# Delta rule: where the inverse's transposed first value is made, and the order of two VectorE steps

## The reference, cut to what matters

```
L = where(strict, (k_beta @ k.T) * decay, 0)
T = triangular_solve(eye + L, eye)                # the inverse of I + L
v_corr = T @ v_beta
k_cumdecay = T @ (k_beta * exp(gc))
attn_intra = where(tril, (q @ k.T) * decay, 0)
# scan over chunks: state, o
o_gdn = rms_norm(o, gdn_out_norm_w) * silu(z)     # the gated output
```

```
qkv = silu(sum(xp[:, i:i+S] * w[i] for i in range(4)))
```

## Time and profile before

| | |
|---|---|
| median of 3 runs | 2905.5 us (2904.29 to 2907.15) |
| profiled execution | 2909.46 us, its span 2907.7 us |
| PE busy | 2759.3 us (95%) |
| DVE busy | 1890.3 us (65%) |
| ACT busy | 1195.7 us (41%) |
| POOL busy | 536.7 us (18%) |
| delta rule | from about 300 to 690 us of the span |

### The profile page before, as it was taken

The page is one execution under the profiler, slowest core; times in us unless marked ns, Lnnn a source line. Parts: engine busy times, 40 slices in busy tenths (PEclk is TensorE's granted clock), DMA queues, the critical chain, the costliest instruction groups (busy, mean ns, idle before and its releaser), DMA issues.

```text
span 2907.7 us, 36988 instructions
## 1 busy us (share of the span) xinstructions
PE 2759.3 (95%) x14045; PEld 2343.5 (81%) x14045; DVE 1890.3 (65%) x3534; ACT 1195.7 (41%) x1928; POOL 536.7 (18%) x393
## 2 busy tenths in 40 slices
PE   8999999989998999999998999999999978999997
PEld 6777878878777999998997888888887546788876
DVE  3334665765565778877975888888885674544434
ACT  5545243233223454447993333333333444422322
POOL 0112220220000787771000111111110021000000
PEclk9999999999999999999999999999999989999999
DMA  4112101003562587765768989998883101222220
GB/s 160 51 51 86 60 30 44 30 30 131 217 217 114 201 300 280 271 236 191 284 231 308 336 319 346 337 350 324 334 304 131 30 30 44 80 97 92 87 102 29
DMA packets 141359, 501.19 MB, mean 172 GB/s; under 512 B 13400, under 2 KB 67072, under 8 KB 111616
## 3 DMA queue, kind: packets, MB, share of 16 engines
q1 hardware_dynamic: 122752, 364.60, 35.0%
q0 software_dynamic: 18432, 134.23, 11.8%
HBM read 450.53 MB, written 48.25 MB: 172 GB/s over the span
## 4 chain that ended last, share of the span: by engine, by line
PE 80%; DVE 9%; ACT 5%; DMA 3%; issue 2%; POOL 1%; SPq 0%; DVEq 0%; ACTq 0%; POOLq 0%
PE bank L244 21%; PE bank L246 21%; PE bank L245 21%; PE bank L2154 2%; DVE xn L1532 1%; PE bank L2743 1%; PE bank L1107 1%; PE bank L740 1%; PE bank L1117 1%; PE bank L1123 1%; DMA w_raw<-in_w_in_dram 1%; DVE M L2946 1%; DVE m L2942 1%; PE bank L346 1%; DVE whl L240 1%
## 5 line engine op out<-in xcount | busy, mean ns | idle before, releaser
L244 PE MATMUL bank<-HH,uhl 128*128 128x384 f32 x1024 | 349.9, 342 | 9.0 <-DVE uhl L1658 7.1
L246 PE MATMUL bank<-HH,uhl 128*128 128x384 f32 x1024 | 346.7, 339 | 0.0
L245 PE MATMUL bank<-HL,uhl 128*128 128x384 f32 x1024 | 346.6, 339 | 0.0
L244 PE MATMUL bank<-vhl,awhl 128*128 128x512 f32 x768 | 300.0, 391 | 6.7 <-DVE awhl L2372 4.7
L246 PE MATMUL bank<-vhl,awhl 128*128 128x512 f32 x768 | 299.8, 390 | 0.0
L245 PE MATMUL bank<-vhl,awhl 128*128 128x512 f32 x768 | 299.5, 390 | 0.0
L1714 POOL DMA_INDIRECT gs<-in_uv_dram,idx x128 | 151.6, 1185 | 776.0 <-DVE x L1739 481.6
L2312 ACT ACTIVATE vhl<-vraw 128x1024 fp32r<-128x1024 f32 x128 | 135.7, 1061 | 317.3 <-PE bank L246 281.8
L1658 POOL TENSOR_TENSOR uhl<-ur,uhl 128x1024 fp32r<-128x1024 f32 x69 | 167.7, 2439 | 321.1 <-ACT uhl L1652 320.8
L244 PE MATMUL bank<-HH,whl 128*128 128x512 f32 x528 | 215.8, 409 | 5.9 <-DVE whl L240 4.1
L240 DVE TENSOR_TENSOR whl<-w_raw,whl 128x2048 fp32r<-128x2048 f32 x49 | 113.5, 2317 | 160.2 <-ACT whl L234 160.1
(11 more groups left out here) (421 smaller groups left out, 6197.3 us busy)
## 6 DMA issues: line engine op xcount, KB each, us to landing
ur<-in_peer_u_dram SPq DMA_DIRECT2D x128, 512.0 KB, 5.5
vraw<-in_peer_v_dram SPq DMA_DIRECT2D x128, 512.0 KB, 5.9
w_raw<-in_w_in_dram SPq DMA_DIRECT2D x36, 1024.0 KB, 5.0
xn<-in_ada_rows_dram SPq DMA_DIRECT2D x48, 512.0 KB, 4.5
g_scratch<-stg SPq DMA_DIRECT2D x12, 2048.0 KB, 8.1
gti<-g_scratch SPq DMA_DIRECT2D x16, 1536.0 KB, 11.5
wf_raw<-in_f_w_in_dram SPq DMA_DIRECT2D x22, 1024.0 KB, 4.8
act_scratch<-ag SPq DMA_DIRECT2D x96, 192.0 KB, 2.7
```

The source lines that it names most:

```text
L244: e.matmul(out, l[0], r[0], start=start, stop=False)
L245: e.matmul(out, l[0], r[1], start=False, stop=False)
L246: return e.matmul(out, l[1], r[0], start=False, stop=stop)
```

## The change

XT's first value is no longer made from LT by GpSimd. In step 3 PE transposes X into a bank of the ring, behind the product of the same head, and ScalarE copies it into XT. GpSimd's two operations for it are gone. The wait for "onw" moves to ScalarE, and step 4's first product waits for ScalarE. In VectorE's order, the first convolution of the next pair goes from step 1 to step 2, behind the six evictions; the gated outputs of the pair before go from step 2 to step 4, behind the updates of X and XT.

```diff
--- before.py
+++ after.py
@@ -1106,8 +1106,15 @@
                 for tb in range(NT):
                     i = e.matmul(b[:, blk(tb)], B["LT"][:, tb, :], B["X"][:, tb, :], start=True, stop=True)
                 i.then_inc(*T.up("p", h, l))
+                if l == 0:
+                    b = R3.take("xT", h)
+                    for s in R3.empty("xT", h):
+                        e.wait_ge(*s)
+                    for tb in range(NT):
+                        i = e.transpose(b[:, blk(tb)], B["X"][:, tb, :], ident)
+                    i.then_inc(*T.up("xT", h))
             else:
-                e.wait_ge(*(V.of("xt", h, l - 1) if l else G.of("XT", h)))
+                e.wait_ge(*(V.of("xt", h, l - 1) if l else A.of("xT", h)))
                 e.wait_ge(*V.of("p", h, l))
                 if l < LV - 1:
                     b = R3.take("x", h, l)
@@ -1176,6 +1183,11 @@
         if seg == 1:
             e.wait_ge(*T.of("lt", h))
             e.activation(B["LT"][:, :, :], in4(R3.bank("lt", h)), ACT.Copy).then_inc(*R3.out(A, "lt", h))
+        if seg == 3:
+            if h >= 2:
+                e.wait_ge(*V.of("onw", h - 2))
+            e.wait_ge(*T.of("xT", h))
+            e.activation(B["XT"][:, :, :], in4(R3.bank("xT", h)), ACT.Copy).then_inc(*R3.out(A, "xT", h))
         if seg == 15:
             e.wait_ge(*T.of("vc", h))
             e.activation(B["L"][:, :, :], in4(R3.bank("vc", h)), ACT.Copy).then_inc(*R3.out(A, "vc", h))
@@ -1274,13 +1286,6 @@
             e.tensor_tensor(B["X"][:, :, :], B["L"][:, :, :], cb("neg1"), ALU.mult).then_inc(*G.up("x0", h))
             e.wait_ge(*G.of("x0", h))
             e.tensor_tensor(B["X"][:, :, :], B["X"][:, :, :], cb("ident"), ALU.add).then_inc(*G.up("X", h))
-        if seg == 1:
-            e.wait_ge(*A.of("lt", h))
-            if h >= 2:
-                e.wait_ge(*V.of("onw", h - 2))
-            e.tensor_tensor(B["XT"][:, :, :], B["LT"][:, :, :], cb("neg1T"), ALU.mult).then_inc(*G.up("xt0", h))
-            e.wait_ge(*G.of("xt0", h))
-            e.tensor_tensor(B["XT"][:, :, :], B["XT"][:, :, :], cb("ident"), ALU.add).then_inc(*G.up("XT", h))
         if seg == 2:
             q = head_q(h)[0]
             e.wait_ge(*V.of("kq", h))
@@ -1351,10 +1356,12 @@
                 for f in range(2):
                     if g and seg == 0:
                         dve_gdn_norm(e, 2 * g - 2 + f)
-                    if g and seg == 2:
+                    if g and seg == 4:
                         dve_gdn_gated(e, 2 * g - 2 + f)
                 if g < 3:
-                    if seg - 1 in STEP:
+                    if seg == 2:
+                        dve_gdn_conv(e, g + 1, STEP[0])
+                    if seg - 1 in STEP and seg > 1:
                         dve_gdn_conv(e, g + 1, STEP[seg - 1])
                     if seg in STEP:
                         dve_gdn_low(e, g + 1, STEP[seg])
```

## The result

| | before | changed |
|---|---|---|
| median (8 runs each) | 2908.05 us | 2893.87 us |
| range of the runs | 2904.3 to 2911.9 | 2886.1 to 2899.0 |
| ratio | | 0.9948, 95% interval 0.9939 to 0.9958 |
| profiled execution, its span | 2909.46, 2907.7 us | 2892.33, 2890.6 us |

The change is 15.1 us faster by the ratio (0.0052 of 2908), 17.1 by the two profiled executions. The forecast was a gain of 9.3, to 2896.2 us. The direction, the place and the stalls were right; one term, the clock, was sized too small. The median lies only 2.3 us under the forecast time because the three runs of before that the forecast started from (2905.5) lay 2.55 us under the median of eight. That part is luck: the gain of 15.1 is above even the largest one that the prediction's sum allowed, 11.74.

What follows compares the result with a forecast made beforehand. PE was taken as the bound, stalled in the delta rule by VectorE's late mask. Gains of 0.79, 3.61, 2.00 and 2.91 us in pairs 0 to 3 sum to 9.31, from 2905.5 to 2896.2 us; range 2892.3 to 2902.5.

Steps and rivals of the forecast that it cites:

- the clock: Step 4 of pairs 1 and 3: falls of granted clock after the stall vanish, gaining 1.62 and 1.46 us.
- The stall and its releaser: Step 4's first product (L1117) waits 12.18 us over four pairs; VectorE's late mask (L1227), not GpSimd's XT, releases it.
- The sizes of the stalls: L1117 waits 1.67, 2.87, 2.88 and 4.76 us; gone in pairs 0 to 2, about 1.7 left in pair 3.
- Transposes: Step 3 on PE: eight added a pair cost 0.88 us, 3.52 in all, counted fully.
- ScalarE's eviction: Step 3: one XT copy of 0.59 us a head, covered by PE's other work if ScalarE is free.
- the later split: ScalarE's split of the next weights comes at most 2.8 us later, covered by VectorE's 3.70 us idleness: 0.
- the bank wait: Step 3: PE's reuse of banks waits for KW and VB evictions; taken as 0, otherwise 0.6 us in pair 3.
- SP: SP's eight o_scratch loads wait for the later gated outputs; first used 51 us after, so 4 us later costs nothing.
- A: First convolution stays slow or VectorE is otherwise as late: gain 6.9 us, 2898.6 us; chance 0.09.
- B: The clock falls in all four pairs after step 3: gain 3.0 us, 2902.5 us; chance 0.08.
- C: A later stage paced by transfers or a fixed chain takes the gain back: 2905.5 us or up to 2 below; chance 0.09.
- D: Clock falls throughout steps 3 and 4, broken by VectorE and bank waits: 19.4 us slower, 2924.9 us; chance 0.04.

## Why the prediction came out as it did

*The stall and its releaser: right.* The chain "convolution, evictions, gated outputs, mask" was VectorE's, and bringing the mask forward by either part was enough. The convolution's 2.83 us without GpSimd beside it, the 1.16 us from product to mask, and PE being the bound in pairs 0 to 2 came as stated.

*The sizes of the stalls: right to half a microsecond.* Pairs 0 and 2 shifted by 1.02 and 2.24 where 0.79 and 2.00 were forecast. About the same 0.24 is missing in both, and 0.17 of it has a source in the rows: idle time starts at the end of the last record, but a record of 1.06 us (L1107 at 424.88) is followed after 0.89 (425.77) when PE doesn't wait. A stall costs its idle time and this overhang. Pair 3: waits of 1.44 and 0.84 where the prediction has about 1.7 and 0.9, and 2.9 of shift as forecast. The 1.7 didn't follow from its own numbers: 4.76, less the 2.35 by which step 4 comes earlier, less 0.88 of transposes, is 1.53.

*Transposes: right.* 0.88 a pair, shown by doubling them.

*ScalarE's eviction, the later split, the bank wait, SP: right at 0.* No wait of PE on any of them is in the trace.

*The step that was mis-sized: the clock.* The sum took 1.62 and 1.46 us for the two falls that the one profile had in step 4, 3.08 in all, and called their coming a matter of chance for stalls of this size. That was right in kind, but the sum then counted what one execution had drawn and not what such stalls draw in the mean. The runs show more: the mean granted clock is 0.9828 for the kernel before (14 runs beside the last timing) and 0.9853 to 0.9854 for the changed one (6 and 8 runs), which is 50.0 and 42.2 us lost, a difference of 7.8 (an upper estimate, as it counts every microsecond at half clock as half lost, also where PE was idle). With 6.6 from stalls this makes 14.4 of the 15.1. I had drawn the rule from one execution, in which two of the four stalls were followed by a fall. Over three, pair 1 has a fall in three, pair 2 in two, pair 3 in three (once a double one), and pair 0, whose stall is 1.67 to 1.88 us, in one. That the waits bring the falls is shown by putting them back, and by the profiles of all kernels together. Step 4 was followed or met by a fall after none of the 8 waits of 1.4 to 1.7 us, after 3 of the 9 of 1.9 to 2.7, after 5 of the 6 of 2.9 and after all 5 of 4.7 and more. So the prediction's reading that a remaining wait of under 1.7 us brings no fall held.

*What stays open.* Of the 7.8, the 3.3 falls of step 4 make 5.6 at 1.7 each. The rest, about 2, lies mostly behind the delta rule, in stages that the change doesn't touch: there, without the last 16 us or so of the execution, which all kernels spend at half clock, the kernel before spends 72, 72 and 78 us at half clock in its three profiles, the changed one 68 and 65. The other kernels without the stalls have 65 to 72, those with stalls left 72 to 79. No run moves only the start of the later stages, so whether this is their position in time or chance isn't settled.

*The range.* 2893.87 lies in it by 1.6 us, and only because its lower end starts from the low median of three. Its most, "all stalls and clock losses gone", took the clock losses from the same one execution. Measured against the eight runs of before, the gain passes it by 3.4 us.

*The rivals.* A (convolution slow) is refuted by the row at 421.98. B and D are refuted: no fall in steps 3 and 4 in two profiles, nor with the transposes doubled; the rule of the Trainium skill on transposes that rival B names shows no cost here. C is refuted: the shift was 11.5 us at 690 us and 17.1 at the end.

## What to carry to other kernels

Price a stall of PE as its idle time, plus the overhang of the record before it, plus its share of clock falls, and take that share from several executions: one profile showed two falls where the mean of three was 3.3. Here the share grew with the wait, from none up to 1.7 us to nearly always at 2.9. Before stacking two edits that shorten the same queue, ask which of them the engine behind still waits for; here the order of VectorE alone was worth the whole change, and no work had to be moved to PE. If two-operand SBUF work of VectorE stands beside GpSimd, moving it elsewhere may only hand the loss to its neighbour.

## What the runs showed of the hardware that I had not expected

Falls of the granted clock (from full to 1.2 GHz) follow waits of PE as short as 1.88 us, in some executions and not in others: step 4 of pair 0, with a wait of 1.88 us, had granted clock 0.60 in the second profile, and 1.00 with 1.67 in the first and third. Stalls of 10.9 us in all cost another 8.4 us this way. And the loss by GpSimd falls on whichever VectorE operation with two SBUF operands stands there: 1.66 instead of 0.75 for the convolution, 1.5 instead of 0.6 for a gated output, nothing for an eviction out of PSUM.
